# Closing the adaptive-modulation sums of a two-block fp32 kernel with a transpose and a reduction on VectorE and one product on TensorE

## The reference

```python
for l in range(DEPTH_2):                                   # 2 layers
    mod_x = (silu(c) @ w_ada[l] + b_ada[l])[:, None, :]    # w_ada[l]: 1024 x 9216
    mod_c = silu(c_ctx) @ w_ada[l] + b_ada[l]
    sh1, sc1, g1, shm, scm, gm, sh2, sc2, g2 = split(mod_x, 9)
    csh1, csc1, cg1, cshm, cscm, cgm, csh2, csc2, cg2 = split(mod_c, 9)
    h = h + 0.5 * g1 * swiglu(rms_norm(h) * (1 + sc1) + sh1, w_ffn1_gate[l], w_ffn1_up[l], w_ffn1_down[l])
    hc = hc + 0.5 * cg1 * swiglu(rms_norm(hc) * (1 + csc1) + csh1, ...)
    # attention with shm, scm, gm and output projection w_out; then ffn2 with sh2, sc2, g2
```

## Time and profile before

| | us |
|---|---|
| median of 3 runs (lowest, highest) | 2193.02 (2192.41, 2195.32) |
| the profiled execution's own time | 2189.74 |
| its span in the profile | 2188.0 |
| PE busy | 2114.1 (97%) |
| DVE busy | 1343.8 (61%) |
| ACT busy | 777.4 (36%) |
| POOL busy | 416.3 (19%) |
| granted TensorE clock, mean | 0.982 of full speed |

### The profile page before, as it was taken

The page is one execution under the profiler, slowest core; times in us unless marked ns, Lnnn a source line. Parts: engine busy times, 40 slices in busy tenths (PEclk is TensorE's granted clock), DMA queues, the critical chain, the costliest instruction groups (busy, mean ns, idle before and its releaser), DMA issues.

```text
span 2188.0 us, 29282 instructions
## 1 busy us (share of the span) xinstructions
PE 2114.1 (97%) x11971; PEld 1806.2 (83%) x11971; DVE 1343.8 (61%) x1767; ACT 777.4 (36%) x1089; POOL 416.3 (19%) x197
## 2 busy tenths in 40 slices
PE   7988999999999999999999999999999998999998
PEld 6976877888888898668988888888888887679998
DVE  6658788587772267775777762366564236765444
ACT  4343467422222232553322222232222223444443
POOL 0010000222221101351222211122221111243432
PEclk9998999999999999999999999999999999999999
DMA  5328788466653345103566543346663335205654
GB/s 167 97 81 275 229 279 281 116 182 173 184 155 93 99 141 152 58 1 97 149 178 183 172 134 94 92 139 189 192 185 100 99 98 159 76 6 152 190 165 145
DMA packets 415035, 314.93 MB, mean 144 GB/s; under 512 B 27551, under 2 KB 373542, under 8 KB 414902
## 3 DMA queue, kind: packets, MB, share of 16 engines
q1 hardware_dynamic: 375344, 237.43, 37.3%
...
HBM read 311.97 MB, written 1.05 MB: 143 GB/s over the span
## 4 chain that ended last, share of the span: by engine, by line
PE 87%; DVE 7%; ACT 3%; DMA 2%; issue 1%; SPq 1%; DVEq 0%; ACTq 0%
PE ps L2094 23%; PE ps L2096 23%; PE ps L2095 23%; PE ps L2276 2%; PE ps L2087 2%; DVE w_lo L1228 2%; ACT w_hi L732 2%; PE ps L2641 1%; PE ps L2642 1%; PE ps L2643 1%; PE ps L2904 1%; DVE st L1942 1%; DMA raw<-in_w_in 1%; PE ps L2866 1%; PE ps L2673 1%
## 5 line engine op out<-in xcount | busy, mean ns | idle before, releaser
L2094 PE MATMUL ps<-u_hi,w_hi 128*128 128x512 f32 (+2 forms) x2112 | 742.3, 351 | 17.1 <-DVE u_lo L1319 7.6
L2096 PE MATMUL ps<-u_hi,w_lo 128*128 128x512 f32 (+2 forms) x2112 | 731.0, 346 | 0.0
L2095 PE MATMUL ps<-u_lo,w_hi 128*128 128x512 f32 (+2 forms) x2112 | 730.9, 346 | 0.0
L1228 DVE TENSOR_TENSOR w_lo<-raw,w_hi 128x2048 fp32r<-128x2048 f32 (+1 forms) x215 | 451.6, 2100 | 290.5 <-ACT w_hi L732 290.4
L732 ACT CAST w_hi<-raw 128x2048 fp32r<-128x2048 f32 (+1 forms) x215 | 374.8, 1744 | 454.6 <-PE ps L2096 392.0
L2094 PEld LDWEIGHTS ps<-u_hi,w_hi 128*128 128x128 f32 x2112 | 403.1, 191 | 69.2 <-DVE w_lo L1228 8.1
L2096 PEld LDWEIGHTS ps<-u_hi,w_lo 128*128 128x128 f32 x2112 | 402.9, 191 | 48.6
L2095 PEld LDWEIGHTS ps<-u_lo,w_hi 128*128 128x128 f32 x2112 | 403.3, 191 | 46.7
L2024 POOL TENSOR_TENSOR hf_lo<-tmp_b,hf_hi 128x512 fp32r<-128x512 f32 (+1 forms) x88 | 240.4, 2732 | 689.8 <-ACT hf_hi L874 689.8
L1247 DVE SCALAR_TENSOR_TENSOR ada_acc<-ada_w,sc_c,ada_acc 128x512 f32<-128x512 f32 x420 | 319.7, 818 | 7.1 <-DMA ada_w<-in_w_ada 1.3
L2094 PE MATMUL ps<-hf_hi,w_hi 128*128 128x512 f32 (+1 forms) x770 | 268.2, 348 | 0.1
...
## 6 DMA issues: line engine op xcount, KB each, us to landing
...
```

The source lines that it names most:

```text
L1228: tt(low, full, high.bitcast(F32), ALU.subtract).then_inc(lo_done.sem, 1)
L2094: mm(acc, w1, m_hi, start=(first and i == 0), stop=False)
L2095: mm(acc, w1, m_lo, start=False, stop=False)
L2096: ins = mm(acc, w2, m_hi, start=False, stop=(last and i == n - 1))
```

## The change

The reduction over partitions is done in three steps in place of 8 (or 4) fp32 products.

1. `ada_fold`, on DVE, right behind the last multiply of a chunk: `nc.vector.transpose` turns the 32x32 blocks of `ada_acc` (128 x 1024, or 128 x 512 with one stream) into slot 1 of `ada_w`; after it, what were 32 partitions lie along the free axis. A reduction over those 32 gives `ada_red` [128, 32 or 16]: in each quadrant of 32 partitions the sum of that quadrant.
2. `ada_sums`, on PE: one product of `ada_red` with a constant matrix `fold` (1 where the partitions are equal modulo 32) sums the four quadrants into all of them.
3. `ada_out`, on DVE: four instructions, one for each quadrant, pick the columns that belong to it.

`fold` is made once at the start by a reduction of the identity. `tmp_a` is no longer used as a second accumulator. The load of quarter 1 of chunk j waits for the fold of chunk j - 1 (which writes its slot), and the reduction waits until PE has read `ada_red` of the chunk before. The table changes too: f1a takes chunks 4 to 11 at 8 quarters in 5 units, f1b 12 and 13 at 2 in 3 units, f2a 17 to 24 and f2b 25 and 26 likewise, layer 1's f1a 27 to 34 at 17 in 10, its f1b 35. The product stands in the unit after the next behind the one in which the chunk was finished.

```diff
-        ADA = {"f1a": (4, 10, 1, 2, 1), "f2a": (17, 10, 1, 2, 1), "l1_f1a": (27, 9, 1, 2, 2)}
+        ADA = {"f1a": (4, 8, 8, 5, 1), "f1b": (12, 2, 2, 3, 0), "f2a": (17, 8, 8, 5, 1), "f2b": (25, 2, 2, 3, 0),
+               "l1_f1a": (27, 8, 17, 10, 2), "l1_f1b": (35, 1, 2, 3, 0)}
...
                 q = 4 * j + quarter
-                need(act, ada_mac, 4 * (q - 1))
+                if quarter == 1:
+                    need(act, ada_folded, j)
+                else:
+                    need(act, ada_mac, 4 * (q - 1))
...
+                if quarter == 3:
+                    ada_fold(j)
+
+            def ada_fold(j):
+
+                r = len(ada_rows(j))
+                turned_acc = ada_w[:, 1, :, :].rearrange("p k n -> p (k n)")[:, 0:r * ADA_COLS]
+                dve.wait_ge(ada_mac.sem, 16 * j + 16)
+                nc.vector.transpose(turned_acc, ada_acc[:, 0:r, :].rearrange("p v n -> p (v n)")).then_inc(ada_turned.sem, 1)
+                dve.wait_ge(ada_turned.sem, j + 1)
+                need(dve, ada_sum, j)
+                nc.vector.reduce_sum(ada_red[:, 0:16 * r], turned_acc.rearrange("p (b i) -> p b i", i=32), AX_X
+                                     ).then_inc(ada_folded.sem, 1)
...
-                tt(mod[:, v, 0:r], ps[:, 4, 0:2 * nj].rearrange("p (t v) -> p t v", v=2)[:, :, 0:r], b_ada[:, v, 0:r],
-                   ALU.add).then_inc(mod_done.sem, 1)
+                for b in range(4):
+                    q = slice(32 * b, 32 * b + 32)
+                    sums = ps[q, 4, 0:16 * r].rearrange("p (v t b) -> p t v b", v=r, b=4)[:, :, :, b]
+                    ins = tt(mod[q, v, 0:r], sums, b_ada[q, v, 0:r], ALU.add)
+                ins.then_inc(mod_done.sem, 1)
...
+            nc.vector.reduce_sum(fold[:, :].rearrange("p (c j) -> p c j", j=32),
+                                 ident.rearrange("p (o a j) -> p o j a", o=1, j=32).to_broadcast([P, 4, 32, 4]), AX_X)
...
             def ada_sums(j):
-                pe.wait_ge(ada_mac.sem, 16 * j + 16)
+                pe.wait_ge(ada_folded.sem, j + 1)
                 need(pe, mod_done, j)
-                for t in range(ADA_COLS // P):
-                    for v in ada_rows(j):
-                        ins = mm(ps[:, 4, 2 * t + v:2 * t + v + 1], ada_acc_of(j)[:, v, P * t:P * t + P], one, start=True, stop=True)
-                ins.then_inc(ada_sum.sem, 1)
+                r = len(ada_rows(j))
+                mm(ps[:, 4, 0:16 * r], fold[:, :], ada_red[:, 0:16 * r],
+                   start=True, stop=True).then_inc(ada_sum.sem, 1)
```

More of the change, by code:

```diff
@@ L177, in program @@
         sc_c = sb("sc_c", [P, KD, 2])
+        fold = sb("fold", [P, P])
+        ada_red = sb("ada_red", [P, 32])
         coef = sb("coef", [P, KD, 2])
@@ L340, in program @@
         ada_mac = signal("ada_mac", 0)
+        ada_turned = signal("ada_turned", 0)
+        ada_folded = signal("ada_folded", 0)
         ada_sum = signal("ada_sum", 0)
@@ L543, in ada_at, with until @@
                 return [(q // 4, q % 4) for q in range(q0, q1)], {1: 0, 3: 1, 4: 2, 8: 3}.get(n)
-            first, chunks, every, each, start = ADA[ada]
-            n -= start
-            if n < 0:
-                return [], None
-            q0 = (n // every) * each
-            work = [(first + q // 4, q % 4) for q in range(q0, q0 + each) if q < 4 * chunks] if n % every == 0 else []
-            c, rest = divmod((n - 1) * each, 4 * every)
-            return work, first + c - 1 if rest == 0 and 1 <= c <= chunks else None
+            first, chunks, quarters, units, start = ADA[ada]
+            def until(n):
+                return min(4 * chunks, max(n - start, 0) * quarters // units)
+            work = [(first + q // 4, q % 4) for q in range(until(n), until(n + 1))]
+            done = until(n - 1) // 4
+            return work, first + done - 1 if done > until(n - 2) // 4 else None
         def ada_tail(ada, n):
@@ L1101, in _ @@
                        before_third=None if last else first_block_root)
-                ffn_down(L["f1b"], None, (f"l{l}b", h2, T2), keep=(14, 15))
+                ffn_down(L["f1b"], "l1_f1b" if last else "f1b", (f"l{l}b", h2, T2), keep=(14, 15))
                 halves_norm(f"l{l}b", l, 3, end_of(L["f1b"]), next_two(L["f1b"]), second=not last)
@@ L1187, in _ @@
                 ffn_up(L["f2a"], L["sig"][1], TQ, FFN_F, hf_hi, None if last else "f2a")
-                ffn_down(L["f2b"], None, ("end2", h2, SEQ) if last else ("l1a", h2, T2), out_row if last else None,
+                ffn_down(L["f2b"], None if last else "f2b", ("end2", h2, SEQ) if last else ("l1a", h2, T2), out_row if last else None,
                          keep=() if last else (14, 15))
@@ L1236, in ada_quarter @@
                 dve.wait_ge(ada_full[slot], 32 * j + 16 * (quarter // 2) + 16)
-                rows, acc = ada_rows(j), ada_acc_of(j)
+                rows, acc = ada_rows(j), ada_acc
                 for kk in range(2):
@@ L1242, in ada_quarter @@
                             if v == 0:
-                                need(dve, ada_sum, j - 1 if 1 <= j <= 3 else j)
+                                need(dve, ada_turned, j)
                             ins = ts(acc[:, v, :], ada_w[:, slot, kk, :], sc_c[:, k, v:v + 1], None, ALU.mult)
@@ L1887, in _ @@
                 gates(l, 0, 0.5)
-                ffn_down(L["f1b"], add_gated(T2), None, keep=2)
+                ffn_down(L["f1b"], add_gated(T2), "l1_f1b" if last else "f1b", keep=2)
                 halves_norm(f"l{l}b", l, 3, "mix", L["f1b"], add_half_down(L["f1b"], f"l{l}b"), next_two(L["f1b"]),
@@ L1997, in _ @@
                 gates(l, 6, 0.5)
-                ffn_down(L["f2b"], add_gated(TQ), None, keep=0 if last else 2)
+                ffn_down(L["f2b"], add_gated(TQ), None if last else "f2b", keep=0 if last else 2)
             n = norm_of["end2"]
@@ L2802, in _ @@
                     ffn_up(L["f1a"], T2, FFN_F, "f1a", n0=1, before_third=first_block_mean)
-                ffn_down(L["f1b"], L["sig"][0], T2, 11, hf_hi, hf_lo, FFN_F, None, f"l{l}b", T2, keep=2)
+                ffn_down(L["f1b"], L["sig"][0], T2, 11, hf_hi, hf_lo, FFN_F, "l1_f1b" if last else "f1b", f"l{l}b", T2, keep=2)
                 close_down(L["f1b"], f"l{l}b", hf_hi, hf_lo, 11)
@@ L2950, in _ @@
                        whole=last)
-                ffn_down(L["f2b"], L["sig"][1], TQ, 11, hf_hi, hf_lo, FFN_F, None,
+                ffn_down(L["f2b"], L["sig"][1], TQ, 11, hf_hi, hf_lo, FFN_F, None if last else "f2b",
                          "end2" if last else "l1a", TQ, turn_out if last else None, keep=0 if last else 2)
```

2 lines of the change are left out of this document (removed).

## The result

| | before | after |
|---|---|---|
| median, us | 2193.4 (2192.4 to 2195.3, 4 runs) | 2177.2 (2176.2 to 2178.0, 4 runs) |
| ratio, 95% interval | | 0.9925 (0.9908 to 0.9942) |
| profiled span, us | 2188.0 | 2176.0 |
| PE records | 11971 | 11531 |

The change gains 16.1 us. Forecast were 36.7, with a range of 2146 to 2173 us: the sign was right, and the time lies 4 us outside the range.

The account below looks back on a forecast made before the run. PE, busy 97% of the span, was taken as the bound. Burst savings of 33.0 + 5.4, experts 3.5 and chunk 15's 1.6, less 6.8 for uncovered folds, gave 36.7 us gain: 2193.0 to 2156.3, range 2146 to 2173.

Parts of the forecast that it names:

- where the fold is covered: Stage by stage, whether DVE's fold makes PE wait; 6.8 us deducted for tails, down units, q and out.
- the signs: Wrong if PE waits mid up unit, a down unit begins over 0.5 us late, or the transpose is far from 1.1.
- The burst and the product: On PE, a lone product of 0.28 us replaces each burst, saving 1.57 us a two-row chunk and 0.68 a one-row chunk.
- F, the fold's length: On DVE, transpose plus reduction at each chunk's end take 2.3 us, bounds 1.9 and 3.5.
- rival 1: On DVE the fold is longer, about 3.4 us, stretched like some multiplies; 2174 us, chance 0.18.
- The quarter in the down units: In f1b and f2b, a 2.7 us quarter within DVE's 7.4 us before w_lo, against PE's 7.48; 0.1 a fold, 0.4 in all.
- Hidden, by 0.1 us: In up units of f1a and f2a, DVE's fold ends at 13.5 us, before PE's product at 13.6; no cost.
- the tails: At the ends of f1a and f2a, PE waits 1.45 us for the fold, twice; costs 2.9 us.
- The expert stage: Chunks 0 to 3: shorter bursts, partly lost to late DVE; gain 3.5 us, bounds -1 and +8.
- q and out: Late w_lo costs 2.3 us at chunk 14 and 1.2 at chunk 16, without burst savings; chunk 15 gains 1.6.
- the start: Building the constant fold matrix takes about 0.6 us beside PE and ACT; costs nothing.
- Rival 3: Up-unit matmuls queue behind a product waiting for DVE's fold; slower than before from F = 4.5 us, 2236 at 6.5; chance 0.04.

Follow-up runs that it names:

- own_buffer: Changed kernel with the turned sums of chunks 4 and on in memory of their own, so ACT's load no longer waits for the fold; 2172.4 us (ratio 0.9894).
- fold_short: Changed kernel with each chunk's transpose and reduction done on one block of 32 columns only, waits and products kept; 2143.7 us (ratio 0.9773).
- experiment 1: The run fold_short: changed kernel with transpose and reduction cut to one block of 32 columns; 2143.7 us, 48.3 less than the old kernel.

## Why the prediction was wrong

What PE was spared came out as forecast. What failed is the part on where the fold is covered, and a term that the sum did not have: the clock after a wait. PE did wait in the middle of up units (0.55 us), and a down unit did begin more than 0.5 us late (1.24), two of the signs that the prediction had named for being wrong.

- **The burst and the product: right.** 0.28 us taken for the lone product, 0.25 measured. 1.57 and 0.68 us saved gave 49.4; fold_short shows 48.3, part of that agreement by chance (experiment 1).
- **F, the fold's length: right to 0.15 us.** 2.30 taken, 2.42 measured from the transpose's start to what follows (1.28 + 1.14). The mistake is not in rival 1, though its time of 2174 is near: a stretch of 1.05 us is there, but in the multiplies ahead of the fold. The fold was never stretched: beside GpSimd (1709.78 to 1711.29) the transpose of 128x512 takes 0.71 as its seven others do. The rule of the Trainium skill (GPSIMD Engine Reference, 1. Specifications), that instructions with two SBUF inputs are hit and those with one are not, agrees with both. The Trainium skill's other page (Vector Engine (DVE) Microarchitecture Reference, 3.8), by which the prediction estimated 1.07 us, agrees in the rate: 1.245 - 0.711 us for 512 more columns is 1.04 ns each.
- **The quarter in the down units: the step that failed there.** "A quarter, 2.7" should have been 3.77, as in two quarters of 6.41 in the earlier trace rows, which are 5.4 and 1.04 from GpSimd. The up units' quarters went into the sum as measured, with GpSimd in them; the down unit's was added up from unstretched multiplies, and in f1b GpSimd adds squares. 7.4 against 7.48 us was a cover of nothing, and with 1.04 and the slower F it became a wait of 1.24 in each of four units and 3.1 us a stage, 6 in all where 0.4 stood.
- **"Hidden, by 0.1 us": the step that failed in the up units.** The wait of ACT for the fold was put at 0.15 us. It made SiLU 0.56 late (459.79 is 11.44 after the one before, a unit is 10.88), and that pushes DVE: the next double unit's quarters (475.45) start 27.10 us after the SiLU at 448.35, in own_buffer 26.65 after the same unit's (446.72 to 473.37). Six waits of 0.55 followed. With the tails, predicted at 1.45 and measured at 2.06, f1a and f2a cost 11.3 instead of 2.9.
- **The expert stage: +3.5 was forecast and -2.6 measured**, outside its own bounds of -1 to +8. The step priced the folds at the places where they meet a wait, three of them, and by fold_short the four folds of 2.42 cost 9.9 instead of the 2.8 in the sum, more than their whole length. How that divides is open: DVE has little idle time there, but the granted clock also stands at 0.50 for 37.5 us of the stage, in fold_short for 27.3 and in the old kernel for 34.1, and no run separates the two.
- **q and out: the folds right, the clock missing.** Together they were forecast 1.9 longer (2.3 + 1.2 - 1.6) and are 5.7. The folds made w_lo late by 2.5 and 1.4, and chunk 15's burst gave 1.5 back, all as forecast. The other 3.4 are two stretches at the lower clock (last section), for which the sum had no term.
- **The tails, the start.** A wait of 2.06 us cost 1.6 more in f1a, again by the clock: from the product to the first add it is 17.12 us there and 15.50 in f2a. The 1.6 us at the start belong to the run.
- **Rival 3** did not come, with this spread and at this length, as reckoned. Its point of 4.5 us was not run. With the old spread the same mechanism makes the kernel slower at 2.4 already, by 36 us.

Against the old kernel's spans the stages were forecast and measured, as us gained: experts 3.5 and -2.6, f1a with f1b 14.05 and 6.7, q with out -1.9 and -5.7, f2a with f2b 14.05 and 8.0, layer 1 7.0 and 7.3, the rest 0 and -1.7. That is 36.7 and 12.0. The medians show 16.1, because the old kernel's profiled execution lies 3.6 us below its median and the changed one's 0.5 above.
